# A chunked triangular inverse inside a two-block model: its turned form by transposes instead of a second update

## What is computed

```
lower = einsum(kb, kc) * decay * (1 - eye)
t_mat = triangular_solve(eye + lower, eye)      # the inverse
u = t_mat @ (vc * bc)
w = t_mat @ (kb * exp(gc))
```

## Time and profile before

| | us |
|---|---|
| runs (three) | 2225.23, 2228.34, 2228.13; median 2228.13 |
| the profiled execution | 2227.45 |
| its span | 2225.7 |
| mean granted clock of TensorE | 0.991 |
| where the two mixers' inverses lie | about 260 to 360, and 850 to 950 |

### The profile page before, as it was taken

How to read it: one execution, slowest core, us unless ns; L and a number is a source line. 1 busy time by engine, 2 the same in 40 slices (tenths; PEclk the granted TensorE clock), 3 DMA queues, 4 the chain that set the end, 5 groups by cost and what they waited for, 6 DMA issues and landing times.

```text
span 2225.7 us, 34909 instructions
## 1 busy us (share of the span) xinstructions
PE 2171.4 (98%) x13019; PEld 1906.2 (86%) x13030; DVE 1653.0 (74%) x2135; ACT 1181.8 (53%) x1589; POOL 67.1 (3%) x70
## 2 busy tenths in 40 slices
PE   8999999999999999999999999999999999999997
PEld 7888999788788889988888888988888888898886
DVE  6877787777777777957777777867887657776657
ACT  5555535655654563455546455546456545646554
POOL 0000200000000002100000000100000000000000
PEclk9999999999999999999999999999999999999999
DMA  8765322477487642127765775435764556434453
GB/s 318 298 247 210 114 76 77 172 291 273 153 323 300 252 156 95 58 76 271 271 256 215 294 277 214 151 116 208 293 253 184 184 197 228 152 106 158 172 190 149
DMA packets 59414, 446.68 MB, mean 201 GB/s; under 512 B 6976, under 2 KB 7360, under 8 KB 8896
## 3 DMA queue, kind: packets, MB, share of 16 engines
q1 hardware_dynamic: 59328, 445.50, 53.7%
HBM read 444.42 MB, written 1.05 MB: 200 GB/s over the span
## 4 chain that ended last, share of the span: by engine, by line
PE 88%; DVE 6%; ACT 3%; issue 1%; DMA 1%; SPq 0%; DVEq 0%; ACTq 0%
PE ps L248 27%; PE ps L357 15%; PE ps L253 14%; PE ps L363 7%; PE ps L264 3%; PE ps L306 2%; PE ps L307 2%; PE ps L312 2%; PE ps L229 1%; PE ps L338 1%; PE ps L230 1%; PE ps L235 1%; DVE w_lo L205 1%; PE ps L1156 1%; PE ps L1168 1%
## 5 line engine op out<-in xcount | busy, mean ns | idle before, releaser
L205 DVE TENSOR_TENSOR w_lo<-raw,w_hi 128x1024 fp32r<-128x1024 f32 x670 | 812.9, 1234 | 302.6 <-ACT w_hi L198 302.0
L198 ACT ACTIVATE w_hi<-raw 128x1024 fp32r<-128x1024 f32 x670 | 694.2, 1052 | 425.5 <-PE ps L363 133.0
L248 PE MATMUL ps<-hT,w_hi 128*128 128x512 f32 x2688 | 671.3, 392 | 0.1
L248 PEld LDWEIGHTS ps<-hT,w_hi 128*128 128x128 f32 x2688 | 487.9, 189 | 91.0 <-ACT w_hi L198 0.6
L253 PEld LDWEIGHTS ps<-hT,w_lo 128*128 128x128 f32 x2688 | 366.7, 190 | 26.2
L253 PE MATMUL ps<-hT,w_lo 128*128 128x256 f32 x2688 | 374.8, 282 | 0.0
L357 PE MATMUL ps<-w_hi,act_hi 128*128 128x512 f32 x672 | 209.0, 392 | 0.0
L357 PE MATMUL ps<-w_hi,act_lo 128*128 128x512 f32 x672 | 207.6, 390 | 0.0
L363 PE MATMUL ps<-w_lo,act_hi 128*128 128x512 f32 x672 | 179.6, 389 | 0.0
L2045 DVE SCALAR_TENSOR_TENSOR arena<-arena,cond 128x1024 f32<-128x1024 f32 x144 | 168.5, 1220 | 2.3 <-DMA arena<-in_w_ada 2.3
L357 PEld LDWEIGHTS ps<-w_hi,act_lo 128*128 128x128 f32 x672 | 126.2, 188 | 27.5
(11 more groups left out here) (366 smaller groups left out, 2552.3 us busy)
## 6 DMA issues: line engine op xcount, KB each, us to landing
raw<-in_u SPq DMA_DIRECT2D x88, 1024.0 KB, 4.9
raw<-in_d SPq DMA_DIRECT2D x88, 1024.0 KB, 6.9
raw<-in_g SPq DMA_DIRECT2D x87, 1024.0 KB, 4.9
arena<-in_w_ada SPq DMA_DIRECT2D x48, 1536.0 KB, 7.5
raw<-in_w_in SPq DMA_DIRECT2D x54, 1024.0 KB, 4.9
raw<-in_w_out SPq DMA_DIRECT2D x16, 1024.0 KB, 4.9
rows<-in_rows SPq DMA_DIRECT2D x12, 1024.0 KB, 9.0
arena<-in_con SPq DMA_DIRECT2D x1, 1344.0 KB, 9.8
```

Source lines behind the costliest of these rows:

```text
L198: nc.scalar.activation(w_hi[:, buf, 0:width], raw[:, slot, half * UNIT:half * UNIT + width], ACT.Copy).then_inc(unit_hi, 1)
L205: nc.vector.tensor_tensor(w_lo[:, buf, 0:width], raw[:, slot, half * UNIT:half * UNIT + width], w_hi[:, buf, 0:width].bitcast(F32), ALU.su ...
L248: nc.tensor.matmul(o, h_[:, k, c], hT[:, :, 4 * half + k, :], start=(half == k == 0), stop=False)
```

## The change

In the first ten steps the update makes only the correction itself (bank 1), and DVE subtracts it from `X` index 0. Two steps later, behind `product(i + 2)`, PE transposes the four new matrices into bank 2 (`turn(i)`), and ACT copies the bank over `X` index 1 (`turned_inverse(i)`). The last two steps make the transposed correction alone, as before, but in bank 1. Two semaphores are new: `inv_t` (a turn is in the bank) and `inv_y` (it is copied). `turn(i)` waits for copy `i - 1`, and `update(i)` for copy `i - 2`. On ACT the ten copies are put into the written order one by one.

```diff
+TURNS = 2 * LEVELS - 2
...
+    inv_p, inv_c, inv_r, inv_x, inv_t, inv_y = (sem(f"inv_{c}") for c in "pcrxty")
...
             last.then_inc(inv_p, 1)
+            if i >= 2:
+                turn(i - 2)
+
+        def turn(i):
+            if i:
+                pe.wait_ge(inv_y, l * TURNS + i)
+            for q in range(4):
+                last = nc.tensor.transpose(ps[:, 2, q * P:(q + 1) * P], x_of(4 * (i % 2) + q, 0), IDENT)
+            last.then_inc(inv_t, 1)
 
         def update(i):
             pe.wait_ge(inv_c, l * 2 * LEVELS + (i + 1))
             if i:
                 pe.wait_ge(inv_x, l * 2 * LEVELS + i)
+            if i >= 2:
+                pe.wait_ge(inv_y, l * TURNS + (i - 1))
             for q in range(4):
                 m_ = 4 * (i % 2) + q
-                if i < 2 * LEVELS - 2:
-                    nc.tensor.matmul(ps[:, 1, q * P:(q + 1) * P], x_of(m_, 1), pm[:, m_, :], start=True, stop=True)
-                last = nc.tensor.matmul(ps[:, 2, q * P:(q + 1) * P], pm[:, m_, :], x_of(m_, 1), start=True, stop=True)
+                left, right = x_of(m_, 1), pm[:, m_, :]
+                if i >= TURNS:
+                    left, right = right, left
+                last = nc.tensor.matmul(ps[:, 1, q * P:(q + 1) * P], left, right, start=True, stop=True)
             last.then_inc(inv_r, 1)
...
+        def turned_inverse(i):
+            a.wait_ge(inv_t, l * TURNS + (i + 1))
+            nc.scalar.activation(X[:, i % 2, 1, :], ps[:, 2, :], ACT.Copy).then_inc(inv_y, 1)
...
         evict(8)
+        turned_inverse(0)
         hi(10, (0,))
+        turned_inverse(1)
         hi(10, (1,))
         softmax_exp(0)
         evict(9)
+        turned_inverse(2)
         hi(11, (0,))
+        turned_inverse(3)
         after(V1, "dec_m")
...
         evict(10)
+        turned_inverse(4)
         hi(12, (0,))
+        turned_inverse(5)
         after(V1, "lam1")
         nc.scalar.activation(lamb[:, 2:4], lamb[:, 0:2], ACT.Exp).then_inc(A1.done("lam"), 1)
         after(T1, "o_m")
...
         hi(12, (1,))
         evict(11)
+        turned_inverse(6)
         hi(13, (0,))
+        turned_inverse(7)
         after(T1, "trans_d")
         nc.scalar.activation(blocks(pT), bank_blocks(3), ACT.Copy).then_inc(A1.done("pT"), 1)
         hi(13, (1,))
         silu_s(range(0, 2), "silu_x")
         hi(14, (0,))
+        turned_inverse(8)
...
         hi(14, (1,))
+        turned_inverse(9)
         silu_s(range(2, 6), "silu_s")
...
         def subtracted(i):
             v.wait_ge(inv_r, l * 2 * LEVELS + (i + 1))
-            z = 0 if i < 2 * LEVELS - 2 else 1
-            nc.vector.tensor_tensor(X[:, i % 2, z:2, :], X[:, i % 2, z:2, :], ps[:, 1 + z:3, :],
-                                    ALU.subtract).then_inc(inv_x, 1)
+            z = 0 if i < TURNS else 1
+            nc.vector.tensor_tensor(X[:, i % 2, z, :], X[:, i % 2, z, :], ps[:, 1, :], ALU.subtract).then_inc(inv_x, 1)
```

More of the change, by code:

```diff
@@ L1054, in build @@
     ones_set = sem("ones_set")
-    inv_p, inv_c, inv_r, inv_x = (sem(f"inv_{c}") for c in "pcrx")
+    inv_p, inv_c, inv_r, inv_x, inv_t, inv_y = (sem(f"inv_{c}") for c in "pcrxty")
     T1 = steps("mix1_t", "narrow sums rows_n kk_even kk qk_even qk x0 rope_t rows_a map00 map01 map02 map03 rows_m map10 map11 "
```

## The result

The change makes the kernel slower by 0.3%: 2233.34 us, the median of ten runs (2230.13 to 2240.11), against 2227.38 for ten of the kernel before (2225.23 to 2230.82). The ratio is 1.0031, with a 95% interval of 1.0018 to 1.0045. The forecast was 2238.0, with 2229 to 2247 around it. The profiled execution of the change took 2231.47 us, with a span of 2229.7.

What follows compares the result with a forecast made beforehand. PE, busy 98%, was taken as the bound, in a chain DVE and ACT must feed in time. To 2227.45 us came +5.2 (waits less saved work) and +5.1 (clock): 2237.8, rounded to 2238.0; range 2229 to 2247.

Steps and rivals of the forecast that it cites:

- The saved work: PE, ten steps: four matmuls (0.90 us) replaced by a turn (0.41); 0.49 saved per step, 4.9 us per layer, 9.7 in all.
- Copy 5: On ACT ahead of `den`: delays DVE's mask, so PE waits 4.6 us before update(7), per layer.
- Rival 1: Work saved and no wait comes, as DVE's tail from `den` to the mask is covered: 2217.7 us, 6%.
- Copy 7: On ACT ahead of the `pT` copy: PE waits 2.25 us before L1177, which needs `pT`, per layer.
- The other eight copies: ACT's remaining copies hold back splits, exponentials and `silu_s` that are due later; taken at no cost.
- w_m: Behind copy 3 and `dec_m`: ready 7.8 us after the turn, PE has 8.3; cost 0, at worst about 2 us.
- The clock: TensorE's clock falls behind both waits: 1.6 us each, 0.65 of it hidden at the first; +2.55 per layer, +5.1 together.
- the wait for L1896: After update(7), `trans_d` needs DVE's L1896, 2.8 us after the mask: PE waits 0.65 us more, per layer.
- the row of 2.6 us idle: Profile row ahead of L2210: after 2.6 us of PE idle, clock 0.83, 3.4 us at 1.2 GHz; basis for 1.6 us.
- rival 2: Both waits come and the clock doesn't fall: +5.2 us, 2232.7 us, 18%.
- rival 4: Waits come, but clock falls at the score maps move away (-3.3, -1.6 us) or waits get none: about 2231 us, 8%.

Runs made afterwards that it cites:

- the second series: The change, unchanged, timed again beside the version with only copy 7 moved on the same chip: 2233.94 us, ratio 1.0034 to the kernel before.

## Why the prediction was right, and where it wasn't

**The saved work.** A turn was put at 0.41 us. In the change it runs from 324.10 to the next unit's start at 324.45 or from 357.97 to 358.41: 0.35 to 0.44. From the update's start to what follows the product, or the turn, a step takes 2.22 us, not 2.68: 0.46 shorter, where 0.49 was forecast; 9 us over both layers. The version with both copies moved bears it out: 9 less twice 1.0 for the two small waits on DVE makes 7, and 7.7 us were measured.

**Copy 5.** Forecast: 4.6 us, with `den` done 1.05 after the turn. Measured: 4.47, DVE's `den` reader at 325.59, 1.14 after the turn's end at 324.45. Moving this one line gave 9.0 us back, the wait and some 3 us of clock. Rival 1, which needed the cover, fell with it.

**Copy 7.** Forecast 2.25, measured 2.12. Its removal is seen in the list of waits and in the first stage, but was worth nothing alone, where the clock took it back, and 4.8 us beside the other.

**The other eight copies** cost nothing that the profiles show; `w_m`, whose margin was put at half a microsecond, appears in no list of waits: in the change it ends at 316.04, and `o_m` starts at 316.75.

**The clock was the mis-sized term.** The sum had +5.1 us: a fall of 1.6 us at each of the four waits, less 0.65 hidden at the larger two. At the larger wait the clock did fall, in ten of ten places in the five profiles that have it unfilled; there the work up to the transposes `trans_d` took 1.7 us longer, some 0.65 us of which would have gone on the wait for L1896 in any case, as forecast. Behind the wait for `pT` it fell in none of the four places of the change's two profiles: these are 3.2 of the 5.1 us, and the row of 2.6 us idle, from which they were taken, didn't carry over. What the step left out is that falls elsewhere change as well. The change has one piece at each group of maps, four in a profile, where the kernel before had three and five; and it was hit behind the gap in one place of four, the kernel before in three of four.

What is left over all executions is told by the mean granted clock: 0.9898 for the 22 of the change, 0.9912 for the 66 of the kernel before. By the slope of 1.9 us per 0.001 that is some 2.6 us, an estimate, half of the forecast term. (The four profiles alone, 9 and 8 pieces before and 7 and 10 after, would say nothing at all; they are too few.) With it the forecast would have been 2227.4 + 5.2 + 2.6 = 2235.2. Measured were 2233.34 and, in the second series, 2233.94, where the kernel before stood at 2226.6: 6.0 and 7.3 us slower.

**How good the forecast was.** Its way was right: both waits, their places and sizes, and the sign. But 2233.34 lies below the range of 2234 to 2242 that the forecast gave for its own case, 0.6 us from the number of rival 2 (2232.7). It is inside 2229 to 2247 because that range takes in the rivals. Rival 2's mechanism, no fall at the waits, is not what the profiles show; nearest to them is rival 4, falls elsewhere that move away, though it was the gap and not the maps that lost them. Rival 4's own terms make 2238 - 3.3 - 1.6 = 2233.1, not the 2231 that it gives.

## What to carry to other kernels

In an order written by hand, a wait that is put on an idle engine is not free: look at what stands behind it in that engine's queue, and how much slack the readers of that have; here two lines out of ten, which cost PE 4.5 and 2.1 us in each layer, turned a gain of 9 us of work into a loss of 6, and moving the first one alone made the kernel 3 us faster than before. When a move of a few microseconds shows nothing, check the granted clock before giving up the theory: compare stages with equal instructions, and the mean clock of all executions rather than the pieces of one profile. Filling a short gap on PE with products of no use kept the clock up behind it in four places of four here, but the gain in time, 1.6 us, isn't shown.

## What the runs showed of the hardware

- 3.4 us at the lower clock level cost 1.5 us where PE is the bound. Over 66 executions of one kernel, 0.001 less of mean granted clock went with 1.9 us.
- A gap of 1.5 us ahead of narrow products (64 columns) let the clock fall in 17 of 24 places, filled with products in none of 4. An idle stretch of 2.1 us between other work let it fall in 2 of 8, both in the version with copy 5 moved; one of 4.5 us in 10 of 10.
- The Trainium skill (TensorE: Matmul & The Clock Gate, Part 4: PE-mode transpose) says that a transpose doesn't count as PE-busy the same way as a matmul. Here four of them ahead of the maps gave the same time as two matmuls, within 0.1 us in the medians, and the same mean clock; the runs don't show the rule, and four transposes are too few to exclude it.
- A float32 transpose of 128x128 is one record of 0.10 to 0.11 us, a float32 matmul of that size two, 0.22 us in all.
